# Attention inside a transformer block: scores once in float32 with two heads on the row halves, exponentials transposed by TensorE, values of two heads side by side

## Chip, cores, metric

One core of one Trainium2 chip. The metric is device time in microseconds of one execution, median over runs.

## What is computed

A transformer block with 512 latent and 256 context tokens, width 1024, then a second block (a long convolution and a convolutional feed-forward). The change touches only the attention of the first one, and the retention that is computed beside it. Heads are 64 wide; eight query heads share two key and value heads; retention has eight heads of its own.

```python
def gqa_block(q, k, v):
    qg = q.reshape(B, Q, ATTN_KV_HEADS, GQA_GROUP, HEAD_DIM)
    s = jnp.einsum('bqkgd,btkd->bkgqt', qg, k) * ATTN_SCALE      # HEAD_DIM ** -0.5
    p = jax.nn.softmax(s, axis=-1)
    o = jnp.einsum('bkgqt,btkd->bqkgd', p, v)
...
# retention, per chunk of 128 tokens
inner = jnp.einsum('bhid,bhjd->bhij', qc, kc) * decay_mat
o = jnp.einsum('bhij,bhjd->bhid', inner, vc) + jnp.einsum('bhid,bhde->bhie', qc, state) * q_decay
...
ret = head_group_norm(ret) * silu(g_r)
out = concatenate([att, ret]) @ w_out
```

All is float32. Queries are the 512 latent tokens, keys and values the 768 of context and latent.

## The kernel before

The kernel is written engine by engine, each engine's instructions in an order fixed by hand, with counting semaphores between engines. Features lie on the 128 partitions, tokens along the free dimension. Two heads share one tile `t` (0 to 3): head `h = 2t + e` has the 64 rows `e*64` to `e*64+63`. One of the two (`e = 0`) belongs to the first key head, the other to the second, so `KA` holds both key heads, one on each half of the rows.

Order of the work. The input projection runs 22 units of weights through TensorE (`latent_part`, L638); queries and keys are turned by the rope on VectorE (L2102 to L2111) as their unit comes. Behind it come three things interleaved.

The retention, per pair `t`: `inner(h)` (L842) makes q·k of one head in four products of 128 columns, K = 64 rows, into bank 4 or 5; `ret_decay(h)` on VectorE (L2134) multiplies by the decays into `pr`; `inter(t)` (L855) adds the state's part; `inner_values(t)` (L864) makes the values of head `2t`, then those of `2t+1`, on 64 columns of the array each, into bank 6 or 7. `ret_out` (ScalarE), `gn_variance` (TensorE, L873), `gn_log`, `gn_root`, `gn_gate`, `gn_scale`, `gn_high`, `gn_low` norm, gate and split the result. `query_decay(t)` (VectorE, L2047) prepares `inter`'s operand.

The attention, per head `h`, makes each score twice. `row_max` (L896, L897) makes scores with queries on the partitions, 128 queries by 768 keys, and VectorE takes the largest of each row (`att_max`, L2152). `att_diagonal` and `shift_row` (L907) turn these 512 maxima into a row over all partitions, which `shift_high` and `shift_low` put as a correction into free rows of the query's low part. `scores(h, kt)` (L918, L919) then makes the shifted scores with keys on the partitions, six tiles of 128 keys by 512 queries. ScalarE takes the exponential (`exponent`, L1424) into `PA` or `PB`, and `values` (L931) multiplies by `V`, whose tile has a block of ones beside the 64 value columns, so that the sum of the exponentials comes out on the other half of the partitions. `inverse_sum` (ln and exp on ScalarE) and `att_scale` divide; `att_high` and `att_low` split the result for the output projection.

The products of `row_max` and `scores` are in the float32r type: keys and queries are split into a high part (float32r) and the rest. `Kst` has the high key part on the head's own rows and the low part on the other rows, `K2` the high part and a constant. The splits are made by ScalarE (L1371 to L1388), VectorE (`key_low` L2036, `query_low` L2143 and L2144) and GpSimd (memsets of the free rows). The products of `values`, `inner`, `inter` and `inner_values` are plain float32.

```python
nc.tensor.matmul(PS[:, 4 + kt % 2, :], Kst[:, e, ks], q_high(t, e), start=True, stop=False)
nc.tensor.matmul(PS[:, 4 + kt % 2, :], K2[:, e, ks], q_low(t, e), start=False, stop=True)
...
nc.tensor.matmul(out_bank(h), V[:, kt, h % 2 * HD:h % 2 * HD + P], p_tile(v), start=kt == 0, stop=kt == 5)
```

In the loop over heads TensorE makes `scores` of head h, `values` two tiles behind, and `row_max` of head h+1 between them. VectorE has modulation rows (L2071) in its gaps. The third thing is the output projection with `w_out` (L638 again, eight units), whose first two units start with the slices that are ready; its weights are split by ScalarE (`split_hi`, L621) and VectorE (`split_lo`, L628).

Elsewhere, the filter of the second block has two products on opposite halves of the rows (`filter_tile`, L708 for one tile, L712 for the others), and `key_transposes` (L778) transposes float32 tiles on TensorE.

Of the kernel before, what the change touches and what calls it, by code (L numbers as in the profile page):

```python
# [122 lines left out]
def build(nc, xT, ctxT, cols, mats, w, rope, rdist, crow, mod_x, mod_w, mod_c, posT, fw, fwout, decay, fwd4, inv, out):  # L123
# [3 lines left out]
    with ExitStack() as stack:  # L127
# [45 lines left out]
        Dg = sb("Dg", o_r + 16 * K + LA // P * VW * 4, [P, 4, P])  # L173
# [15 lines left out]
        QS1 = sb("QS1", o_r, [P, 2, 2, L], F32R)  # L189
        R = sb("R", o_r + 8 * K, [P, 2, L])  # L190
        Kst = sb("Kst", o_r + 75 * K, [P, 2, LA], F32R)
        K2 = sb("K2", o_r + 81 * K, [P, 2, LA], F32R)
# [11 lines left out]
        PA = sb("PA", o_r + 38 * K, [P, 6, L])  # L204
        PB = sb("PB", o_t, [P, 6, L])
# [48 lines left out]
        def sem(name):  # L254
# [49 lines left out]
        a_kh, a_kl, a_qh, a_ql = sem("a_kh"), sem("a_kl"), sem("a_qh"), sem("a_ql")  # L304
        a_s, a_mx, a_dg, a_row, a_mh, a_ml = (sem("a_s"), sem("a_mx"), sem("a_dg"), sem("a_row"), sem("a_mh"),
                                              sem("a_ml"))
        a_st, a_exp, a_pv, a_r, a_o, a_h, a_lo = (sem("a_st"), sem("a_exp"), sem("a_pv"), sem("a_r"), sem("a_o"),
                                                  sem("a_h"), sem("a_lo"))
        a_zero = sem("a_zero")
# [137 lines left out]
        def q_high(t, e):  # L447

            return H[:, 0, 2 + e, :] if t % 2 == 0 else QS1[:, 0, e, :]

        def q_low(t, e):

            return H[:, 1, 2 + e, :] if t % 2 == 0 else QS1[:, 1, e, :]

        def p_tile(v):

            return PA[:, v % 12, :] if v % 12 < 6 else PB[:, v % 12 - 6, :]

# [200 lines left out]
        def _(pe):  # L659
# [170 lines left out]
            def inner(h):  # L830

                t, lo = h // 2, h % 2 * HD
                if h == 0:
                    pe.wait_ge(q_done, NROPE - 1)
                elif h == 1:
                    pe.wait_ge(q_done, NROPE)
                else:
                    pe.wait_ge(r_p, h - 1)
                if h % 2 == 0:
                    pe.wait_ge(q_done, rope_count(NQR + t) + 1)  # L840
# [17 lines left out]
            def inner_values(t):  # L858

                for e in range(2):  # L860
                    h = 2 * t + e
                    pe.wait_ge(r_p, h + 1)
                    for c in range(4):
                        mm = nc.tensor.matmul(PS[e * HD:(e + 1) * HD, 6 + t % 2, c * P:(c + 1) * P],  # L864
                                              V[:, c, 3 * HD + h * HD:3 * HD + (h + 1) * HD],
                                              pr[:, h % 2, c * P:(c + 1) * P], start=False, stop=c == 3)
                    mm.then_inc(r_pv, 1)
# [8 lines left out]
            def row_max(h, qt):  # L876

                t, e, u = h // 2, h % 2, 4 * h + qt
                if u == 0:
                    pe.wait_ge(a_kh, 6)  # L880
                if qt == 0:
                    pe.wait_ge(a_zero, h + 1)
                    pe.wait_ge(a_ql, h + 1)
                    pe.wait_ge(a_qh, h + 1)
                if u == 0:
                    pe.wait_ge(a_kl, 2)
                    pe.wait_ge(q_ev, 22)
                elif u == 1:
                    pe.wait_ge(s_st, 8)
                    pe.wait_ge(k_dec, 6)  # L890
                else:
                    pe.wait_ge(a_mx, u - 1)
                qs = slice(qt * P, (qt + 1) * P)
                for a, b, bank in ((0, L, 0), (L, LA, 1)):
                    ps = PS[:, 2 * (qt % 2) + bank, 0:b - a]
                    nc.tensor.matmul(ps, q_high(t, e)[:, qs], Kst[:, e, a:b], start=True, stop=False)  # L896
                    mm = nc.tensor.matmul(ps, q_low(t, e)[:, qs], K2[:, e, a:b], start=False, stop=True)  # L897
                mm.then_inc(a_s, 1)

            def shift_row(h):  # L900

                pe.wait_ge(a_dg, h + 1)
                if h:
                    pe.wait_ge(a_exp, 6 * h - 1)
                else:
                    pe.wait_ge(r_p, 8)
                nc.tensor.matmul(PS[:, 4, :], ones[:, :], Dg[:, :, :].rearrange("p a b -> p (a b)"), start=True,  # L907
                                 stop=True).then_inc(a_row, 1)

            def scores(h, kt):  # L910

                t, e, v = h // 2, h % 2, 6 * h + kt
                if kt == 0:
                    pe.wait_ge(a_ml, h + 1)
                if v >= 2:
                    pe.wait_ge(a_exp, v - 1)
                ks = slice(kt * P, (kt + 1) * P)
                nc.tensor.matmul(PS[:, 4 + kt % 2, :], Kst[:, e, ks], q_high(t, e), start=True, stop=False)  # L918
                nc.tensor.matmul(PS[:, 4 + kt % 2, :], K2[:, e, ks], q_low(t, e), start=False,  # L919
                                 stop=True).then_inc(a_st, 1)  # L920

            def values(h, kt):

                v = 6 * h + kt
                pe.wait_ge(a_exp, v + 1)
                if kt == 0:
                    if h < 2:
                        pe.wait_ge(g_ln, 3 + h)
                    else:
                        pe.wait_ge(a_o, h - 1)  # L930
                nc.tensor.matmul(out_bank(h), V[:, kt, h % 2 * HD:h % 2 * HD + P], p_tile(v), start=kt == 0,  # L931
                                 stop=kt == 5).then_inc(a_pv, 1)

            inner(0)
            inter(0)
            inner(1)
            inner(2)
            inner_values(0)
            inner(3)
            row_max(0, 0)  # L940
            for t in range(1, NPAIR):
                inter(t)
                gn_variance(t - 1)
                if t < 3:
                    inner(2 * t + 2)
                    inner_values(t)
                    inner(2 * t + 3)
                    row_max(0, t)
                else:
                    row_max(0, t)  # L950
                    inner_values(t)
            shift_row(0)
            gn_variance(3)
            row_max(1, 0)
            for h in range(8):
                scores(h, 0)
                scores(h, 1)
                if h < 7:
                    row_max(h + 1, 1)
                for kt in range(2, 6):  # L960
                    values(h, kt - 2)
                    scores(h, kt)
# [1829 lines left out]
```

## Time and profile before

| | |
|---|---|
| device time, three runs | 1436.34 us (1435.34 to 1437.79) |
| span of the profiled execution, first to last instruction | 1433.4 us |
| instructions in it | 16730 |
| TensorE, VectorE, ScalarE, GpSimd busy | 1379.9, 923.8, 536.4, 93.9 us |
| mean granted TensorE clock | 0.989 of full |

The profiled execution's own time is recorded only as its span; the device times of the runs above take in what lies before the first and behind the last instruction. Times in the trace are counted from the start of the span. A product with float32 operands appears as two MATMUL instructions, each with its own weight load (PEld).

### The profile page before, as it was taken

The numbers are of one execution on the slowest core, as the hardware profiler recorded it, in microseconds if no ns is written. First come the engines' busy times: TensorE is split into PE (matmuls) and PEld (weight loads), VectorE is DVE, ScalarE is ACT, GpSimd is POOL, SyncE is SP. The second block draws the span as 40 slices with busy tenths as digits, with TensorE's granted clock in tenths as the row PEclk, the third lists the DMA queues.
The fourth block names the chain that finished last, engine by engine and source line by source line (L and its number), as shares of the span: only waits on it lengthen the run. The fifth ranks groups of instructions, "written<-read, shape, count | busy, mean of one in ns | idle before, by whom it ended". The sixth has DMA issues, their size and how long they took to land.

```text
span 1433.4 us, 16730 instructions
## 1 busy us (share of the span) xinstructions
PE 1379.9 (96%) x6174; PEld 1090.4 (76%) x6174; DVE 923.8 (64%) x1245; ACT 536.4 (37%) x764; POOL 93.9 (7%) x110
## 2 busy tenths in 40 slices
PE   7899999999979999999999999999999999999996
PEld 5688887666748888888887477778887888888885
DVE  6855687785266666655232896999477888785222
ACT  3423353554352232232222654433454333433221
POOL 0002630000300000000110000000110000000010
PEclk9899999999989999999999999999999999999999
DMA  9424330032217666664521021220222322333211
GB/s 383 157 93 153 115 110 23 30 103 89 88 54 247 214 218 214 213 237 172 172 91 63 30 88 65 83 103 30 88 74 82 97 100 88 102 115 105 101 61 59
DMA packets 44801, 168.80 MB, mean 118 GB/s; under 512 B 5547, under 2 KB 6123, under 8 KB 43852
## 3 DMA queue, kind: packets, MB, share of 16 engines
q1 hardware_dynamic: 43340, 165.21, 33.6%
q0 software_dynamic: 1408, 2.89, 0.7%
q8 instruction: 33, 0.54, 0.2%
q14 instruction: 20, 0.16, 0.0%
HBM read 163.09 MB, written 2.10 MB: 115 GB/s over the span
## 4 chain that ended last, share of the span: by engine, by line
PE 84%; DVE 10%; ACT 2%; SPq 2%; issue 1%; DMA 1%; DVEq 0%; ACTq 0%
PE PS L638 68%; PE PS L931 2%; DVE wsp L628 1%; PE PS L1107 1%; DVE tb L1869 1%; DMA wraw<-w_w_in 1%; PE PS L1204 1%; PE PS L1175 1%; PE PS L724 1%; DVE H L1869 1%; PE PS L652 1%; PE PS L896 1%; SPq L516 1%; DVE ca L1869 1%; PE PS L995 1%
## 5 line engine op out<-in xcount | busy, mean ns | idle before, releaser
L638 PE MATMUL PS<-H,wsp 128*128 128x512 f32 x3408 | 786.5, 391 | 12.2 <-DVE wsp L628 8.8
L638 PEld LDWEIGHTS PS<-H,wsp 128*128 128x128 f32 x3408 | 635.9, 188 | 156.5 <-issue 12.0
L628 DVE TENSOR_TENSOR wsp<-wraw,wsp 128x1024 fp32r<-128x1024 f32 (+1 forms) x180 | 233.0, 1295 | 374.8 <-ACT wsp L621 374.1
L621 ACT ACTIVATE wsp<-wraw 128x1024 fp32r<-128x1024 f32 (+1 forms) x180 | 200.5, 1115 | 507.3 <-PE PS L638 494.4
L638 PE MATMUL PS<-hid,wsp 128*128 128x512 f32 x1056 | 240.0, 389 | 0.0
L638 PEld LDWEIGHTS PS<-hid,wsp 128*128 128x128 f32 x1056 | 198.1, 188 | 41.8 <-issue 0.6
L1869 DVE SCALAR_TENSOR_TENSOR cva<-PS,dert,cva 128x441 f32<-128x441 f32 (+2 forms) x176 | 122.2, 695 | 5.5
L2071 DVE CUSTOM_DVE_ANT_0 sink<-mring,crow_t,colt 128x1024 bf16<-128x1024 f32 x56 | 71.7, 1280 | 0.4
L1803 POOL COPY acc<-sqb 128x512 f32<-128x512 f32 x4 | 4.4, 1093 | 867.5 <-ACT sqb L1248 306.9
L1806 POOL TENSOR_TENSOR acc<-acc,sqb 128x512 f32<-128x512 f32 x23 | 40.8, 1773 | 193.7 <-ACT sqb L1781 82.6
L1524 ACT ACTIVATE hid<-hv 128x512 f32 (+1 forms) x22 | 13.9, 632 | 71.3 <-DVE hv L2299 71.3
L2152 DVE TENSOR_REDUCE dert<-PS 128x1 f32<-128x768 f32 x32 | 29.9, 951 | 9.3 <-PE PS L897 9.2
L1760 ACT ACTIVATE sl<-cva,colt 128x512 f32<-128x512 f32 x22 | 15.9, 725 | 50.5 <-DVE cva L1869 50.5
L724 PE MATMUL PS<-sqb,ones 128*128 128x512 f32 (+1 forms) x48 | 26.7, 719 | 7.9 <-ACT sqb L1248 7.9
L1817 POOL DMA_DIRECT2D RS<-RU x44 | 21.8, 502 | 171.9 <-ACT RU L1347 135.5
L1869 DVE SCALAR_TENSOR_TENSOR ca<-cb__148,colt,ca 128x512 f32<-128x512 f32 x40 | 30.0, 749 | 1.2 <-ACT ca L1606 0.5
L638 PEld LDWEIGHTS PS<-Hc,wsp 128*128 128x128 f32 x240 | 30.0, 192 | 0.7
L638 PE MATMUL PS<-Hc,wsp 128*128 128x256 f32 x240 | 30.2, 283 | 0.0
L652 PE MATMUL PS<-H,wsp 128*128 128x512 f32 x96 | 25.7, 429 | 4.1 <-DVE H L1869 4.1
L1869 DVE SCALAR_TENSOR_TENSOR H<-tb,dert,H 128x512 fp32r<-128x512 f32 (+1 forms) x40 | 24.7, 640 | 6.6 <-ACT H L1710 4.1
L1204 PE MATMUL PS<-invt,KS 128*128 128x256 f32 x128 | 28.1, 380 | 0.7 <-DVE KS L2474 0.7
L1248 ACT ACTIVATE sqb<-X 128x512 f32<-128x512 f32 x30 | 18.7, 627 | 26.6 <-DMA X<-xT 9.2
(307 smaller groups left out, 1361.4 us busy)
## 6 DMA issues: line engine op xcount, KB each, us to landing
mring<-mod_c SPq DMA_DIRECT2D x56, 512.0 KB, 4.7
wraw<-w_ffn_in SPq DMA_DIRECT2D x44, 512.0 KB, 3.6
wraw<-w_up SPq DMA_DIRECT2D x44, 512.0 KB, 3.4
wraw<-w_hy_in SPq DMA_DIRECT2D x24, 512.0 KB, 3.4
wraw<-w_w_in SPq DMA_DIRECT2D x22, 512.0 KB, 3.6
wraw<-w_ffn_out SPq DMA_DIRECT2D x16, 704.0 KB, 4.0
wraw<-w_down SPq DMA_DIRECT2D x16, 704.0 KB, 4.1
mfirst<-mod_x SPq DMA_DIRECT2D x12, 512.0 KB, 16.4
```

The lines of the kernel that those rows point to most:

```text
L621: nc.scalar.activation(split_parts(name, i, r)[0], wraw[:, g % RAW, 0:n], ACT.Copy).then_inc(w_hi, 1)
L628: nc.vector.tensor_tensor(part_lo, wraw[:, g % RAW, 0:n], part_hi.bitcast(F32), ALU.subtract).then_inc(w_lo, 1)
L638: mm = nc.tensor.matmul(psum, wsp[:, o % 2, a, wk * P:(wk + 1) * P], h[:, b, kt, :], start=first and kt == kts[0] and (a, b) == (0, 0), st ...
L652: mm = nc.tensor.matmul(psums[u], wsp[:, (o + u) % 2, a, kt * P:(kt + 1) * P], h[:, b, kt, :], start=kt == 0 and (a, b) == (0, 0), stop=kt ...
L724: nc.tensor.matmul(PS[:, bank, 0:n], ones[:, :], sqb[:, q % 2, 0:n], start=kt == 0, stop=kt == KT - 1).then_inc(n_acc, 1)
L931: nc.tensor.matmul(out_bank(h), V[:, kt, h % 2 * HD:h % 2 * HD + P], p_tile(v), start=kt == 0, stop=kt == 5).then_inc(a_pv, 1)
L1204: mm = nc.tensor.matmul(PS[:, inverse_bank(j), par * 256:(par + 1) * 256], spectrum(j // 4, f, a)[:, (j % 4) * P:(j % 4 + 1) * P], invt[:, ...
L1806: PL.tensor_tensor(acc_of(k), acc_of(k), sqb[:, q % 2, 0:n], ALU.add).then_inc(n_acc, 1)
L1817: ins = pool.dma_start(moved_tile(n)[to:to + HALF, :], RU[of:of + HALF, n % 2, 0:L])
L1869: return VE.scalar_tensor_tensor(out=o, in0=a, scalar=s, in1=b, op0=op0, op1=op1)
L2071: VE.tensor_tensor_reduce((sink_w if m - 16 < MOD_W else sink)[:, :], unit, crow_t[:, which, :], 1.0, bias, ALU.mult, ALU.add, to).then_in ...
L2152: VE.tensor_reduce(der("mx", u), PS[:, b:b + 2, :].rearrange("p a b -> p (a b)")[:, 0:LA], mybir.AxisListType.X, ALU.max).then_inc(a_mx, 1)
```

## The change

Scores are made once, with queries on the partitions. There are 16 steps; step `s` is pair `t = s // 4` and one tile of 128 queries, for both heads of the pair. `scores(s)` makes four float32 products of K = 64 rows, alternating between the two halves of the rows, into banks 0 to 3. `att_max` gives the negated maximum, which goes as the bias into the exponential; ScalarE sums the exponentials in the same instruction (`accum_out`). `transposes` turns the 2 x 6 tiles of exponentials by TensorE, four at a time, into bank 4 or 5, from where `evict` copies them to `PT` (ScalarE the first and third four, VectorE the second). `values(s)` multiplies for both heads, alternating between column halves, 12 products of 128 columns. `inverse_row` spreads the reciprocals of the sums over the 64 rows of each head by eight products with the identity; `inverse_copy` and `att_scale` apply them. `inner(t)` and `inner_values(t)` of the retention now take both heads of a pair, alternating as well. The factor 1/8 of the scores is put into the last product of the query's rope. All splits of keys and queries, the shift rows and GpSimd's memsets go. The whole diff of the orders of work is long; its core:

```diff
-            def inner(h):
-                t, lo = h // 2, h % 2 * HD
-                if h == 0:
-                    pe.wait_ge(q_done, NROPE - 1)
-                elif h == 1:
+            def inner(t):
+                if t == 0:
                     pe.wait_ge(q_done, NROPE)
                 else:
-                    pe.wait_ge(r_p, h - 1)
+                    pe.wait_ge(r_p, 2 * t)
                 for c in range(4):
-                    mm = nc.tensor.matmul(PS[:, 4 + h % 2, c * P:(c + 1) * P], KR[lo:lo + HD, t, c * P:(c + 1) * P],
-                                          QR[lo:lo + HD, t, c * P:(c + 1) * P], start=True, stop=True)
+                    for e in range(2):
+                        rows, _ = head_rows(e)
+                        mm = nc.tensor.matmul(PS[:, 4 + e, c * P:(c + 1) * P], KR[rows, t, c * P:(c + 1) * P],
+                                              QR[rows, t, c * P:(c + 1) * P], start=True, stop=True)
                 mm.then_inc(r_s, 1)
...
             def inner_values(t):
-                for e in range(2):
-                    h = 2 * t + e
-                    pe.wait_ge(r_p, h + 1)
-                    for c in range(4):
+                pe.wait_ge(r_p, 2 * t + 2)
+                for c in range(4):
+                    for e in range(2):
...
-            def row_max(h, qt):
...
+            def scores(s):
+                t, qs = step_of(s)
+                if s == 0:
                     pe.wait_ge(q_ev, 22)
                     pe.wait_ge(s_st, 8)
                     pe.wait_ge(k_dec, 6)
                 else:
+                    pe.wait_ge(a_exp, 2 * s)
                 for a, b, bank in ((0, L, 0), (L, LA, 1)):
+                    for e in range(2):
+                        rows, _ = head_rows(e)
+                        mm = nc.tensor.matmul(PS[:, 2 * e + bank, 0:b - a], QA[rows, t, qs], KA[rows, a:b],
+                                              start=True, stop=True)
                 mm.then_inc(a_s, 1)
+            def transposes(s, j):
+                i = 3 * s + j
+                pe.wait_ge(a_exp, 2 * s + (1 if j == 0 else 2))
+                if i < 2:
+                    pe.wait_ge(r_p, 8)
+                elif j == 0:
+                    pe.wait_ge(a_td, s)
                 else:
+                    pe.wait_ge(a_ta, 2 * s + j - 1)
+                for b in range(4):
+                    e, kt = (4 * j + b) // 6, (4 * j + b) % 6
+                    tr = nc.tensor.transpose(PS[:, 4 + i % 2, b * P:(b + 1) * P],
+                                             Pq[:, (2 * s + e) % 4, kt * P:(kt + 1) * P], ident[:, :])
+                tr.then_inc(a_tp, 1)
+            def values(s):
+                t, qs = step_of(s)
+                pe.wait_ge(a_ta, 2 * s + 2)
+                pe.wait_ge(a_td, s + 1)
...
+                for kt in range(6):
+                    for e in range(2):
+                        rows, _ = head_rows(e)
+                        mm = nc.tensor.matmul(PS[rows, 6 + t % 2, qs], V[:, kt, 2 * e * HD:(2 * e + 1) * HD],
+                                              PT[:, s % 2, 6 * e + kt, :], start=kt == 0, stop=kt == 5)
+                mm.then_inc(a_pv, 1)
+            def inverse_row(t):
+                pe.wait_ge(a_rec, t + 1)
...
+                for qt in range(4):
+                    for e in range(2):
+                        rows, _ = head_rows(e)
+                        mm = nc.tensor.matmul(PS[rows, 6 + (t + 1) % 2, qt * P:(qt + 1) * P],
+                                              step_col(2, 4 * t + qt, e).to_broadcast([P, HD]), ident[:, :],
+                                              start=True, stop=True)
+                mm.then_inc(a_row, 1)
...
             inner(0)
+            scores(0)
             inter(0)
             for t in range(1, NPAIR):
+                inner(t)
+                inner_values(t - 1)
                 inter(t)
                 gn_variance(t - 1)
+            inner_values(3)
+            for s in range(NSTEP):
+                if s + 1 < NSTEP:
+                    scores(s + 1)
+                for j in range(3):
+                    transposes(s, j)
+                if s == 0:
+                    gn_variance(3)
+                else:
+                    values(s - 1)
+                    if s % 4 == 0:
+                        inverse_row(s // 4 - 1)
+            values(NSTEP - 1)
+            inverse_row(3)
```

ScalarE and VectorE:

```diff
+            def exponent(s, e):
+                act.wait_ge(a_mx, 2 * s + e + 1)
+                if s >= 2:
+                    act.wait_ge(a_tp, 3 * (s - 2) + 2 + e)
+                SC.activation(Pq[:, (2 * s + e) % 4, :],
+                              PS[:, 2 * e:2 * e + 2, :].rearrange("p a b -> p (a b)")[:, 0:LA], ACT.Exp,
+                              bias=step_col(0, s, e), accum_out=step_col(1, s, e)).then_inc(a_exp, 1)
+            for s in range(NSTEP):                                   # ScalarE
+                evict(s, 0)
+                if s + 1 < NSTEP:
+                    exponent(s + 1, 0)
+                    exponent(s + 1, 1)
+                evict(s, 2)
...
+            def att_max(s, e):
+                dve.wait_ge(a_s, s + 1)
+                VE.tensor_reduce(step_col(0, s, e), PS[:, 2 * e:2 * e + 2, :].rearrange("p a b -> p (a b)")[:, 0:LA],
+                                 mybir.AxisListType.X, ALU.max, negate=True).then_inc(a_mx, 1)
...
             ret_decay(0)
-            query_decay(1)
             ret_decay(1)
-            query_low(0, 0)
+            att_max(0, 0)
+            att_max(0, 1)
             ret_decay(2)
...
+            for s in range(NSTEP):                                   # VectorE
+                if s + 1 < NSTEP:
+                    att_max(s + 1, 0)
+                    att_max(s + 1, 1)
+                evict(s, 1)
...
+                if 1 <= s <= 12:
                     modulation_row(next(mod_next))
```

`query_decay(1)` moves to just behind the last rope product; `split_hi` of w_out's units 0 and 1 to the ends of steps 14 and 15 on ScalarE.

## Rows read from the trace of the kernel before

**Rows 1.** The page, busy time and share of the span of each engine.

```profile
PE 1379.9 (96%) x6174; PEld 1090.4 (76%) x6174; DVE 923.8 (64%) x1245; ACT 536.4 (37%) x764; POOL 93.9 (7%) x110
```

**Rows 2.** Stretches: length, then each engine's busy time, granted clock, DMA.

```profile
227.66:258.25 30.59, 30.33 (x222) 24.87 (x222) 23.33 (x35) 10.58 (x18) 1.04 (x2) 1.00 0.01 2
258.25:349.20 90.95, 89.27 (x317) 54.54 (x316) 67.94 (x94) 49.88 (x84) 2.07 (x4) 1.00 0.23 76
```

**Rows 3.** The chain of waits: start us, us, what.

```profile
236.16 1.78 PE PS L855 x16
...
238.81 1.08 PE PS L842 x8
239.89 1.51 PE PS L864 x16
...
258.51 0.24 PE PS L918
...
260.12 0.86 PE PS L931 x2
...
349.78 10.24 PE PS L638 x45
```

**Rows 4.** Instructions in order of time near 773: start us, us, engine, line.

```profile
772.89 0.59 PE L708 MATMUL PS<-fwo,fz 128*128 128x512 f32 x1
773.41 0.31 PEld L712 LDWEIGHTS PS<-fwo,feat 64*128 64x128 f32 x1 [0.76 <-issue]
773.41 0.82 PE L712 MATMUL PS<-fwo,feat 64*128 64x512 f32 x1
...
773.42 0.81 PE L712 MATMUL PS<-fdif,feat 64*128 64x512 f32 x1
...
774.07 0.59 PE L712 MATMUL PS<-fwo,feat 64*128 64x512 f32 x1
774.07 0.59 PE L712 MATMUL PS<-fdif,feat 64*128 64x512 f32 x1
...
774.59 0.50 PE L638 MATMUL PS<-hid,wsp 128*128 128x512 f32 x1
```

**Rows 5.** Instructions in order of time near 155, TensorE.

```profile
154.68 0.60 PE L778 MATMUL PS<-ident,KR 128*128 128x128 f32 x4
```

**Rows 6.** Groups by line and form, 220 to 352: busy us, mean ns, idle before.

```profile
L2152 DVE TENSOR_REDUCE dert<-PS 128x1 f32<-128x768 f32 x32 | 29.9, 951 | 9.3 <-PE PS L897 9.2
...
L2071 DVE CUSTOM_DVE_ANT_0 sink<-wraw,crow_t,colt 128x1024 bf16<-128x1024 f32 x12 | 15.4, 1279 | 0.2
L1424 ACT ACTIVATE PA<-PS 128x512 f32<-128x512 f32 x24 | 13.9, 598 | 16.2 <-PE PS L919 15.3
...
L2134 DVE TENSOR_TENSOR pr<-PS,Dm 128x512 f32<-128x512 f32 x8 | 5.5, 688 | 4.8 <-PE PS L864 3.1 <-PE PS L842 1.6
...
L1401 ACT ACTIVATE gsq<-PS,colt 128x512 f32<-128x512 f32 x4 | 2.8, 689 | 10.6 <-PE PS L873 10.6
...
L621 ACT ACTIVATE wsp<-wraw 128x1024 fp32r<-128x1024 f32 x2 | 2.1, 1049 | 0.0
...
L2071 DVE DVE_READ_ACCUMULATOR2_ANT dert<- 128x1 f32 x12 | 1.0, 80 | 0.0
```

**Rows 7.** Instructions in order of time, 224 to 230.

```profile
224.42 1.97 PE L759 MATMUL PS<-RU,swap 128*128 128x512 f32 x4
...
227.63 0.95 DVE L2036 TENSOR_TENSOR Kst<-KA,Kst 64x768 fp32r<-64x768 f32 x1
...
227.66 1.16 PE L842 MATMUL PS<-QR,KR 64*128 64x128 f32 x8 [1.26 <-DVE QR L2105]
...
229.94 0.69 DVE L2105 TENSOR_TENSOR QR<-QR,RM 128x512 f32<-128x512 f32 x1
```

**Rows 8.** Stretches as in rows 2, at a long idle stretch of TensorE.

```profile
397.30:401.50 4.20, 0.00 (x0) 0.03 (x1) 2.82 (x5) 2.89 (x4) 0.00 (x0) 1.00 0.00 0
402.40:409.00 6.60, 5.99 (x8) 2.37 (x8) 6.60 (x12) 3.54 (x6) 0.00 (x0) 0.50 0.00 0
```

More of the change, by code:

```diff
@@ L445, in head_rows, with step_of, step_col @@
             return slice(e * HD, (e + 1) * HD), slice((1 - e) * HD, (2 - e) * HD)
[L447 to L457, printed above, removed]
+        NSTEP = 16
+        def step_of(s):
+            return s // 4, slice(s % 4 * P, (s % 4 + 1) * P)
+        def step_col(which, s, e):
+            k = 8 * (s // 4) + 4 * e + s % 4
+            return stat[:, which, k:k + 1]
         def out_bank(t):
@@ L898, in row_max @@
                 mm.then_inc(a_s, 1)
[L900 to L904, printed above, removed]
-                else:
[L906 to L920, printed above, removed]
@@ L952, in _ @@
[L952 to L962, printed above, removed]
-                    if h < 7 and kt < 4:
-                        row_max(h + 1, kt)
-                if h < 7:
-                    shift_row(h + 1)
-                values(h, 4)
-                values(h, 5)
-                if h < 6:
-                    row_max(h + 2, 0)
@@ L1436, in att_high @@
             def att_high(t):
-                act.wait_ge(a_o, 2 * (t + 1))
+                act.wait_ge(a_o, t + 1)
                 SC.activation(H[:, 0, t, :], R[:, t % 2, :], ACT.Copy).then_inc(a_h, 1)
-            query_high(0)
-            for e in range(2):
-                _, other = head_rows(e)
-                SC.activation(K2[other, e, :], KA[other, :], ACT.Identity, scale=0.0,
-                              bias=colt[other, COL["sel"]:COL["sel"] + 1]).then_inc(a_kh, 1)
+            exponent(0, 0)
@@ L1446, in _ @@
+            exponent(0, 1)
             ret_out(0)
@@ L2030, in _ @@
             state_count = [0]
-            def key_low(e):
-                rows, other = head_rows(e)
-                dve.wait_ge(a_kh, e + 1)
-                VE.tensor_tensor(Kst[other, e, :], KA[rows, :], Kst[rows, e, :].bitcast(F32),
-                                 ALU.subtract).then_inc(a_kl, 1)
             def query_decay(t):
@@ L2136, in ret_decay @@
                                  Dm[:, h, :].unsqueeze(1).to_broadcast([P, 4, P]), ALU.mult).then_inc(r_p, 1)
-            def query_low(t, *only):
-                for e in only or range(2):
-                    rows, other = head_rows(e)
-                    dve.wait_ge(a_qh, 2 * t + e + 1)
-                    VE.tensor_copy(q_high(t, e)[other, :], QA[rows, t, :])
-                    VE.tensor_tensor(q_low(t, e)[rows, :], QA[rows, t, :], q_high(t, e)[rows, :].bitcast(F32),
-                                     ALU.subtract).then_inc(a_ql, 1)
```

284 lines of the change are left out of this document (81 added, 203 removed).

## The prediction

> **What bounds the kernel now.** I read the page's busy times first: TensorE is busy for 96% of the span [rows 1], which does not yet say that its work sets the end of this stage. So next the stretches: from the first retention product at 227.66 to the first attention score at 258.25 TensorE is busy 30.33 of 30.59 us, from there to the output projection at 349.20 for 89.27 of 90.95, while VectorE has 67.94, ScalarE 49.88, and the granted clock is 1.00 [rows 2]. Then the chain of waits, which gives a rate for each form. A float32 product comes as two passes: a value product of 512 columns takes 0.86 us (two passes of 0.43), a float32r score product 0.24, the 16 passes of `inter` 1.78, the 8 of one head's `inner` 1.08, the 16 of `inner_values` 1.51 [rows 3]; the shift row and the variance are each one float32 product of 512 columns, 0.86 again. The loop is TensorE's own work: per head 12 score products (2.8 us), 6 value products (5.2), 16 products for the maxima (about 2.7, those of 256 columns at half price) and the row (0.9) make 11.6 us, times 8 is 92 against 91 seen. Hence what matters is the TensorE time of the new loop, and whether another ring becomes longer than it.
>
> **Where the halves stand in the trace.** Two forms decide. For row halves: `filter_tile` (L712) issues two K=64 float32 products on opposite halves of the rows. Their first passes start at 773.41 and 773.42, their second ones both at 774.07 [rows 4]: the two heads together cost what one costs. For column halves: in `inner_values` (L864) the second head follows the first, and 16 passes of 128 columns take 1.51 us where the 16 of L855, on the whole array, take 1.78 [rows 3]: they overlap where the heads meet, though they come one after the other. Alternating, as the change has it, they should overlap throughout. I take full overlap for both. A change of shape costs: L712's first pass is 0.82 us long against 0.59 and its load comes 0.09 after the stream of L708 ends (772.89 + 0.43), so 0.32; back to the full array, from 774.07 + 0.43 to 774.59 plus 0.107 for the first load (128 columns, as long as such a pass), is 0.20 [rows 4]. Into the 128x64 shape I take 0.15 (bounds 0.1 and 0.3).
>
> The Trainium skill (TensorE: Matmul & The Clock Gate, Part 3) says that matmuls start and end strictly in program order. By it the second head's first pass could not start before the first head's second one; the row pair above shows otherwise, so the sum goes by the row, and the rule is a rival below.
>
> **One step of the new loop, on TensorE.** There are 16 steps, each for two heads and 128 queries.
> - Scores: two passes of 512 and two of 256 columns for both heads at once: 2 x 0.427 + 2 x 0.213 = 1.28, with 0.32 to change shape.
> - Twelve transposes. Those of L778 are one pass each, four in 0.60 us with 0.165 of pipeline end, so 0.11 each [rows 5]: 3 x 0.43 = 1.3, with 0.20 to change shape.
> - Values: 12 products, 24 passes of 0.107, two at a time: 1.28, with 0.15.
> - A wait: the third four go to the bank that ScalarE must first clear of the first four. ScalarE's copy is of the length of L1424, 0.60 [rows 6]; with the end of the pipe and a semaphore (0.2) it is done 0.5 to 0.6 after the second four. So 0.55.
>
> Sum 1.60 + 0.20 + 1.3 + 0.55 + 0.15 + 1.28 = 5.1 us.
>
> **The ring beside it.** `scores(s+2)` waits for both exponentials of step s+1, these for the maxima, these for `scores(s+1)`. Counted from the end of the values before: scores done 1.60 + 0.17; the maxima are 0.95 each (L2152), the second ends at 3.65. The exponential of 768 columns is not in the trace: 0.60 for 512 (L1424), 0.22 for 256 more (half of 1.049 - 0.598, L621 with 1024 against L1424), 0.09 for a bias column (L1401 against L1424) make 0.91 [rows 6]. The first starts after ScalarE's copy at 2.95; they follow each other at some 0.8, the pipe's end overlapping, so the second ends at 4.7, and scores could start at 4.75 where values end at 5.1. So 0.35 us of cover. The sum of the exponentials through `accum_out` on ScalarE has no row. Below it is nothing; above it is one more ScalarE instruction of 0.60 each. The nearest kind is VectorE's read of its accumulator, 0.08 (L2071's second row), so I take 0.1 to 0.2 each, which the 0.35 hides. From 0.2 on, every 0.1 adds 0.2 us per step.
>
> VectorE per step: two maxima 1.8, one copy (between 0.60 as ScalarE's L1424 and 0.69 as L2134, both of 512 columns out of PSUM; I take 0.6), a modulation row 1.36, one more 0.69: 4.5 in 5.1, in an order in which the next maximum comes 0.6 later than VectorE is free. ScalarE: 2 x 0.9 + 2 x 0.55 + 0.6 to 1.06 = 4.0. Both lie beside. If VectorE's work grew by more than 0.6, the maximum would be late and the ring with it.
>
> **Loop and its ends.** Step 0 has no values but a variance product: 4.7. Steps 1 to 14: 14 x 5.1 = 71.4. Three inverse rows inside, 16 passes two at a time, 0.86 each: 2.6. Step 15 without scores, the last values and the last inverse row: 0.2 + 0.86 + 0.5 + 0.45 + 0.15 + 1.28 + 1.28 + 0.86 and a change, 5.8. Together 84.5 against 90.95 now. The output projection's first seven slices (42 products at 10.24/45 each, 9.6 us) still cover the last scaling and splitting, about 3 us of four short instructions, and the wait for w_out's third unit comes behind them as before.
>
> **The stage before the loop.** Removed from TensorE: five groups of products for maxima, 5 x 0.7, and the shift row, 1.0. Moved in: `scores(0)`, 1.3. `inner` is now 16 passes with alternating halves; with 128-column passes (0.11 each, L855) the loads may bind: a load of L712 lasts 0.31 beside its twin, where a lone pass waits only 0.11, so loads may share a port [rows 4]. So 1.75 for two heads instead of 2.2 (bounds 0.9 if loads overlap too, and 2.2). `inner_values`: 0.9 plus 0.15 instead of 1.51. Per pair: 1.8 + 1.05 + 1.9 + 0.9 plus changes of shape, about 5.9 instead of 7.2. VectorE's decays (2 x 0.69, L2134) lie under `inter` and the variance product; ScalarE's two exponentials of step 0 run before `ret_out(0)` and end before it is due.
> But the start moves back: `inner(0)` now covers both heads and waits for the last rope product. Without the key split (0.95 at 227.63) that ends 0.95 before 229.94 + 0.69, at 229.7, not 227.66 [rows 7]: 2.0 lost. From there `inner(0)` 1.8, `scores(0)` 1.5, `inter(0)` 1.9, three rounds of 5.9 and `inner_values(3)` 1.2 end at 253.8, so `scores(1)` starts at 254.0, where 258.25 stands now. Gain 4.3, with the 2.0 taken off.
> The key and query splits, memsets, diagonals and shifts leave ScalarE, VectorE and GpSimd; GpSimd's cost nothing, since nothing else waits behind them before the next norm, and the others lay beside TensorE. The scaled last product of the query rope is one instruction as before, at most 0.06 longer, four times, under the projection. No DMA is moved; w_out's first units wait for modulation rows, now one a step up to step 12 and so done near 320, over 10 us before they are needed.
>
> **Sum.** TensorE would start w_out at 254.0 + 84.5 = 338.5, and its first full pass now begins at 349.78 [rows 3]: 11.3 us less. What follows is unchanged. On the profiled span: 1433.4 - 11.3 = 1422.1. That span lies 2.9 below the median 1436.34 of the three runs, so I forecast 1436.3 - 11.3 = 1425.
>
> **The clock.** TensorE would stand idle from 226.4 to 229.7, 3.3 us. In this trace an idle stretch of 4.2 us was followed by 0.50, the lower level of 1.2 GHz, for the whole stretch after [rows 8], while after 1.26 us idle before 227.66 it stayed at 1.00 [rows 2, 7]. 3.3 is between. If the clock falls, half of the 6.6 us that it stayed down there is lost at most: 3.3. I give it 1 in 4; it stays in the forecast's own range, 1420 to 1430.
>
> **Rivals.**
> - The exponentials bound the ring. With 0.5 us for each accumulation a step is 4.6 + 2 x 0.5 = 5.6, 15 x 0.5 = 7.6 more: 1433. Against it is only that the nearest row is short. It would be slower than before above 0.62 each. Chance 0.13, of which 0.08 still ends below 1433.5, 0.02 within 0.2%, 0.03 above.
> - Program order holds between halves. The first long pass of scores then runs alone, 0.43 per step, 6.5 in all: 1431.5. The row pair speaks against it: 0.05. (By that rule of the skill this is what would happen.)
> - The halves do not run side by side in these forms. Scores alone in line cost 1.28 more in each of 16 steps, 20.5: 1445.5; values too: 1466. It decides from 0.7 us lost per step. For it: L842 and L864 show no alternating heads, and the order of issue differs. Against it: rows 3 and 4. Chance 0.10.
> - It does what it says and moves nothing, since something else sets the start of w_out (its weights, VectorE's two splits): 1436. The cover worked out above speaks against it: 0.05.
> - The forecast: 0.67.
>
> Range: the low end is the forecast with loads of `inner` overlapping too (4 x 0.9 = 3.6 less) and a step a tenth shorter; the high end takes in the order rival, most of the exponential rival and no change: 1420 to 1436, with some 0.13 left out. Within 0.2%, 2.9 us, a measurement of this kernel cannot tell from no change. Faster: 0.67 + 0.05 + 0.08 = 0.80; same: 0.05 + 0.02 = 0.07; slower: 0.10 + 0.03 = 0.13.
>
> **What would show it.** Right: L712-like pairs of starts in scores and values, a step of 5.1 us, TensorE waiting some 0.5 us on ScalarE's copy before the third four transposes and nowhere else, `scores(1)` near 254, w_out near 338. Wrong: scores waiting on ScalarE's exponential (accumulation too dear), scores longer than 1.5 or values longer than 1.5 (no overlap), a granted clock of 0.50 behind 229.7, w_out waiting for its weights.

## The result, and the profile after

| | before | changed |
|---|---|---|
| device time, median | 1435.84 us (4 runs) | 1420.72 us (1419.0 to 1421.17, 4 runs) |
| span of the profiled execution | 1433.4 us | 1419.1 us |
| instructions | 16730 | 17635 |

The ratio is 0.9887, 95% interval 0.9875 to 0.9900; the two medians by themselves give 0.9895 and differ by 15.1 us. The forecast was 1425, a ratio of 0.9921 to the 1436.3 it was worked out from, outside that interval. The direction and the loop's mechanism were right; the gain came out a third larger than the 11.3 us forecast, and the time stands at the low edge of the range. The price of `inner` was wrong, as shown below.

The changed kernel's stretches, with the same columns as [rows 2]: TensorE's wait for the last rope product, the time after it at the lower clock, the rest of the stage before the loop, and the loop.

```profile
228.61:231.90 3.29, 0.00 (x0) 0.00 (x0) 3.12 (x6) 0.00 (x0) 0.00 (x0) 0.94 0.00 0
231.98:234.90 2.92, 2.92 (x20) 2.41 (x22) 1.94 (x4) 0.00 (x0) 0.00 (x0) 0.50 0.02 6
234.94:253.70 18.76, 18.76 (x190) 14.75 (x188) 12.14 (x19) 9.21 (x17) 0.00 (x0) 1.00 0.00 1
253.73:336.07 82.34, 76.42 (x763) 55.15 (x763) 61.30 (x88) 53.18 (x108) 0.00 (x0) 1.00 0.29 91
```

The loop is 82.34 us long where [rows 2] have 90.95. The positions cannot be compared directly: in this execution the projection ended 2.2 us later than in that of before, for reasons far ahead of the change. TensorE's first product began at 10.32 instead of 9.44, and the clock was low once more for 3.4 us near 54 us. Counted from the last swap product of the projection (its last pass plus 0.43: 226.2 before, 228.4 after), the loop begins 25.2 us later instead of 32.0, and the loop itself is 8.6 shorter: 15.4 us in all. What comes after w_out's start takes 1084.2 before and 1083.0 after. The marks are good to some 0.4 us: a pass is marked as started while the one before still runs, and by w_out's second pass (349.85 before, 336.34 after) the gain is 15.7.

The chain of waits of the changed kernel, from the rope products to the first step, and one ordinary step. L833 is `inner`, L880 `scores`, L846 `inter`, L856 `inner_values`, L865 the variance, L896 the transposes, L1390 ScalarE's copy, L915 `values`, L929 the inverse row.

```profile
231.98 2.08 PE PS L833 x16
234.06 1.79 PE PS L880 x8
235.85 1.98 PE PS L846 x16
237.83 1.09 PE PS L833 x16
238.92 1.02 PE PS L856 x16
239.94 1.98 PE PS L846 x16
241.93 0.86 PE PS L865 x2
...
283.94 1.49 PE PS L880 x8
285.43 0.60 PE PS L896 x4
286.03 0.02 issue
286.05 0.61 ACT PT L1390
286.66 0.14 issue
286.79 0.63 PE PS L896 x4
287.42 1.46 PE PS L915 x24
288.88 1.49 PE PS L880 x8
```

A step is 288.88 - 283.94 = 4.94 us, 5.1 forecast. `inner` takes 1.09 for two heads, against 1.08 for one in [rows 3]; only the first takes 2.08, at the lower clock. `inner_values` takes 1.02 against 1.51.

Step 0 is the exception: behind it `scores(2)`, at 258.26, follows ScalarE's exponentials in the chain, and step 0 takes 4.53 (4.7 forecast). The last two steps with what follows them take 10.8 (325.25 to 336.07; 10.9 forecast).

The groups that have no row in the trace of before, and the maxima (columns as in [rows 6]):

```profile
L2072 DVE TENSOR_REDUCE stat<-PS 128x1 f32<-128x768 f32 x32 | 29.1, 952 | 17.5 <-PE PS L880 17.5
...
L1380 ACT ACTIVATE Pq<-PS,stat 128x768 f32<-128x768 f32 x32 | 28.4, 899 | 9.5 <-DVE stat L2072 9.5
L896 PE MATMUL PS<-ident,Pq 128*128 128x128 f32 x192 | 27.5, 280 | 5.7 <-ACT PT L1390 5.7
...
L880 PEld LDWEIGHTS PS<-KA,QA 64*128 64x128 f32 x128 | 11.4, 192 | 11.2 <-issue 10.2 <-ACT Pq L1380 1.0
...
L2081 DVE COPY PT<-PS 128x512 f32<-128x512 f32 x16 | 10.9, 680 | 1.5 <-PE PS L896 1.5
...
L1380 ACT ACTIVATION_READ_ACCUMULATOR Pq<-PS,stat 128x1 f32 x32 | 6.6, 205 | 0.0
```

TensorE's idle time in the loop is the wait for ScalarE's copy, 5.7 us in all, some 0.35 in each of 16 steps. The exponential is 0.90 (0.91 estimated), the accumulator costs one more instruction of 0.205 (0.1 to 0.2 taken). The weight loads of `scores` take 0.192 on average: L712's took 0.31 [rows 4], and it was by L712 that I had priced two terms.

### The profile page after: what moved, and what is told of

Its sections match the earlier page's. It is cut to its first block, busy times and chain, and to the rows that moved or that the text cites. A ratio compares the mean times of both kernels' runs of the same rounds, so it can differ in the third digit from the quotient of the medians.

```text
span 1419.1 us, 17635 instructions
## 1 busy us (share of the span) xinstructions
PE 1361.1 (96%) x6606; PEld 1085.9 (77%) x6606; DVE 907.4 (64%) x1227; ACT 531.9 (37%) x778; POOL 89.8 (6%) x102
## 4 chain that ended last, share of the span: by engine, by line
PE 85%; DVE 10%; ACT 3%; issue 2%; DMA 1%; SPq 0%; DVEq 0%; ACTq 0%
PE PS L632 69%; PE PS L880 2%; PE PS L915 2%; DVE wsp L622 1%; PE PS L718 1%; PE PS L896 1%; DVE tb L1808 1%; PE PS L1092 1%; PE PS L1189 1%; PE PS L1160 1%; DMA X<-xT 1%; PE PS L646 1%; DVE H L1808 1%; DVE ca L1808 1%; PE PS L980 1%
## 5 line engine op out<-in xcount | busy, mean ns | idle before, releaser
L632 PE MATMUL PS<-H,wsp 128*128 128x512 f32 x3408 | 787.8, 392 | 12.3 <-DVE wsp L622 8.8
L632 PEld LDWEIGHTS PS<-H,wsp 128*128 128x128 f32 x3408 | 637.0, 188 | 156.6 <-issue 11.1
L632 PE MATMUL PS<-hid,wsp 128*128 128x512 f32 x1056 | 240.0, 389 | 0.0
L632 PEld LDWEIGHTS PS<-hid,wsp 128*128 128x128 f32 x1056 | 198.1, 188 | 41.7 <-issue 0.6
L2072 DVE TENSOR_REDUCE stat<-PS 128x1 f32<-128x768 f32 x32 | 29.1, 952 | 17.5 <-PE PS L880 17.5
L896 PE MATMUL PS<-ident,Pq 128*128 128x128 f32 x192 | 27.5, 280 | 5.7 <-ACT PT L1390 5.7
L1380 ACT ACTIVATE Pq<-PS,stat 128x768 f32<-128x768 f32 x32 | 28.4, 899 | 9.5 <-DVE stat L2072 9.5
L896 PEld LDWEIGHTS PS<-ident,Pq 128*128 128x128 f32 x192 | 20.4, 140 | 14.2 <-issue 14.2
L632 PEld LDWEIGHTS PS<-Hc,wsp 128*128 128x128 f32 x240 | 30.0, 192 | 0.7
L632 PE MATMUL PS<-Hc,wsp 128*128 128x256 f32 x240 | 30.2, 283 | 0.0
```

Of the source, the lines that this page charges most:

```text
L632: mm = nc.tensor.matmul(psum, wsp[:, o % 2, a, wk * P:(wk + 1) * P], h[:, b, kt, :], start=first and kt == kts[0] and (a, b) == (0, 0), st ...
L896: tr = nc.tensor.transpose(PS[:, 4 + i % 2, b * P:(b + 1) * P], Pq[:, (2 * s + e) % 4, kt * P:(kt + 1) * P], ident[:, :])
L1380: SC.activation(Pq[:, (2 * s + e) % 4, :], PS[:, 2 * e:2 * e + 2, :].rearrange("p a b -> p (a b)")[:, 0:LA], ACT.Exp, bias=step_col(0, s, ...
L2072: VE.tensor_reduce(step_col(0, s, e), PS[:, 2 * e:2 * e + 2, :].rearrange("p a b -> p (a b)")[:, 0:LA], mybir.AxisListType.X, ALU.max, neg ...
```

## The experiments

"By stage" below means two durations, read from each profile by the rule used above: from the projection's last swap product to `scores(1)` ("before the loop", 25.2 in the changed kernel), and from there to w_out ("loop", 82.3). Each duration is from one profiled execution. Ratios are to the kernel before, on the same chip.

### Does the overlap hang on the order of issue?

**Scores head by head.** The change's order is undone in one place:

```diff
-                for a, b, bank in ((0, L, 0), (L, LA, 1)):
-                    for e in range(2):
-                        rows, _ = head_rows(e)
+                for e in range(2):
+                    rows, _ = head_rows(e)
+                    for a, b, bank in ((0, L, 0), (L, LA, 1)):
```

> The four score products of a step are issued head by head (head 0: 512 and 256 columns, then head 1) instead of alternating. Alternation theory: the overlap of the row halves hangs on the order of issue; head 1 starts behind head 0's four passes, scores take 1.49 + 1.28 = 2.8 us, a step 6.2 instead of 4.95, the kernel is some 19 us longer (1440). Look-ahead theory: TensorE starts the passes of the other half as soon as they are in its queue, as head 1 of L864 did in the trace of before after five of head 0's eight passes; scores stay within 1.5 to 1.9 us and the time within 0 to 6 us of the changed kernel's 1420.7.

Measured: 1420.05 us, ratio 0.9885 (0.9869 to 0.9902), the changed kernel's. The loop takes 82.4. In TensorE's order of time both heads' first passes are there at once, in one row:

```profile
287.03 0.71 PE L880 MATMUL PS<-KA,QA 64*128 64x512 f32 x2
```

For the scores the order of issue is worth nothing, as the look-ahead theory had it.

**Scores in line.** Head 1 waits for the end of head 0.

```diff
+                    if e == 0:
+                        mm.then_inc(a_half, 1)
+                        pe.wait_ge(a_half, s + 1)
```

> As by head, and head 1 also waits on a semaphore for the end of head 0's last product, so nothing can overlap. Both theories: scores 2 x 1.28 plus the shape change 0.2 plus pipe end and semaphore 0.3, some 3.1 us against 1.49, 16 x 1.6 = 25 us longer, 1446. It prices the overlap of the row halves: if it is well under 25, something else than TensorE sets the step (ScalarE's exponentials end 0.40 before the scores begin, and would then have to be the reason).

Measured: 1449.83, ratio 1.0091 (1.0074 to 1.0108), slower than before. The chain has two pieces where there was one:

```profile
290.96 1.50 PE PS L881 x4
292.46 0.04 issue
292.50 1.55 PE PS L881 x4
```

The loop takes 106.4, 24.1 more. The other 5.0 lie before the loop, where `scores(0)` is in line too and the clock was low for 10.2 us. So the overlap of the row halves, not the order, carries more than the whole gain: without it the change loses.

**Values head by head.** `for e` outside `for kt` in `values`.

> The 12 value products of a step are issued head by head (6 of head 0, then 6 of head 1). Alternation theory: 24 passes of 0.107 in line, 2.57 + 0.15 = 2.7 us against 1.46, a step 6.2, 20 us longer, 1440. Look-ahead theory: head 1 starts after about five of head 0's twelve passes, so (5 + 12) x 0.107 = 1.8 plus 0.15, some 2.0 us against 1.46, 0.5 a step, 8 us longer, 1429.

Measured: 1434.59, ratio 0.9987 (0.9977 to 0.9997), nearly all the gain gone. The chain shows 2.38 us for the 24 passes instead of 1.46:

```profile
290.48 2.38 PE PS L915 x24
```

In equal columns as [rows 2] (TensorE alone), the number of passes under way in the first 0.89 us of them and in 0.41 after:

```profile
290.41:291.30 0.89, 0.89 (x8) 1.00 0.00 0
291.34:291.75 0.41, 0.41 (x10) 1.00 0.00 0
```

Eight passes start in line, one each 0.11. Head 1's first pass (at 291.34, with the longer duration of a first load) starts together with head 0's ninth, when head 0, with 12 passes, has three left to start. From there two start in each 0.11 until head 0 is through, and head 1's last eight are alone again. In L864 of the trace before, of which [rows 3] give only the total of 1.51, head 1 starts with head 0's fifth of eight, again with three left:

```profile
239.82:240.31 0.49, 0.49 (x5) 1.00 0.00 0
240.31:240.69 0.38, 0.38 (x9) 1.00 0.00 0
```

And a head of `scores` has only four passes, so the other starts with its first. One description fits all three: TensorE starts a pass of the other half at most three passes ahead of its turn. Here neither theory's size was right: I expected 5 + 12 slots, it was 8 + 12. For values the alternation is needed and worth 14.2 us of the loop (96.5).

**Retention head by head.** The same in `inner` and `inner_values`.

> Only the retention's products (inner and inner_values) are issued head by head again. My prediction had 1.8 us for an alternating pair of inner because the weight loads were thought to share a port; the trace of after shows 1.09. If the loads of the two row halves run at once only when they alternate, inner goes to 1.09 x 2 = 2.0 and inner_values from 1.02 to 1.5: 4 x 1.4 = 5.7 us longer, 1426. Look-ahead theory: inner loses half of that or less, inner_values 0.4 each: 2 to 4 us longer, 1423 to 1425.

Measured: 1426.69, ratio 0.9924 (0.9907 to 0.9940); before the loop 30.9 instead of 25.2.

```profile
240.12 1.64 PE PS L833 x16
241.76 1.51 PE PS L856 x16
```

1.64 for 1.09 and 1.51 for 1.02: in both, head 1 starts with head 0's fifth of eight passes, three left. Of the 5.7 us, 4 x 1.04 = 4.2 are these. The clock was low for 6.8 us instead of 3.4 in this execution. Values by head above and values between below, whose stage before the loop is the changed kernel's, also had 6.8 us and both took 26.5 there, 1.2 to 1.3 more than 25.2; that accounts for most of the rest.

### What the wait for the rope costs

**Filler.** Three unused products are put into the wait.

```diff
+            pe.wait_ge(q_ev, 22)
+            for x in range(3):
+                nc.tensor.matmul(PS[:, 2, :], ones[:, :], QA[:, 0, :], start=True, stop=True)
             inner(0)
```

> Three float32 products of 512 columns (0.86 each, results never read) are put in front of inner(0), where TensorE waits 3.4 us for the last rope product. Nothing else changes. Clock theory: the half clock that the trace of after shows from 231.5 on comes from that idle stretch; with it filled the granted clock stays 1.00 there, inner(0) takes 1.09 instead of 2.08 and scores(0) 1.49 instead of 1.79, 1.3 us less (1419.4). Rival: the clock falls for another reason or at random; it falls here too, and the time stays at 1420.7.

Measured: 1417.26, ratio 0.9874 (0.9857 to 0.9891). The clock stays up, with TensorE idle for less than 1 us:

```profile
225.50:229.70 4.20, 3.43 (x8) 1.16 (x7) 4.01 (x7) 0.00 (x0) 0.00 (x0) 1.00 0.00 0
229.74:250.00 20.26, 20.26 (x206) 16.02 (x206) 14.13 (x22) 9.16 (x17) 0.00 (x0) 1.00 0.01 2
```

`inner(0)` takes 1.16 and `scores(0)` 1.29 in its chain, 2.45 instead of 3.87; before the loop 23.8, 1.4 less. That is the clock's price. The medians' difference of 3.5 is larger, but the intervals overlap, so it is the 1.4 that I hold to.

**Scores first.** `scores(0)` and `inter(0)` go in front of `inner(0)`.

> scores(0) and inter(0), which need nothing of the last rope product, are issued before inner(0) and fill the idle stretch of 3.4 us. Start theory: 3.4 us of TensorE work move into the gap and the clock stays up; inner(1) then waits about 1.5 us for VectorE's decays, so 3 us less than now (1417.5), scores(1) starts some 3 us earlier after the end of the projection. Rival: the stage before the loop is held by VectorE's order (decays, maxima, query_decay), and under 1 us comes out.

Measured: 1415.34, ratio 0.9865 (0.9845 to 0.9885); before the loop 22.0, 3.2 less, of which 1.4 are the clock's, which stays up here too. The second `inner` now waits for VectorE's decays, 1.3 us:

```profile
228.43 1.98 PE PS L846 x16
230.41 1.12 PE PS L833 x16
231.53 0.02 issue
231.55 1.30 DVE pr L2065 x2
```

### What sets the step

**Values between.** `values(s-1)` goes between the second and third transposes.

```diff
-                for j in range(3):
-                    transposes(s, j)
+                transposes(s, 0)
+                transposes(s, 1)
+                values(s - 1)
+                transposes(s, 2)
```

> values(s-1) is issued between the second and the third four transposes of step s. The wait of 0.54 us for ScalarE's copy is then covered, at the price of one more change of shape, 0.2. Wait theory: a step goes from 4.95 to 4.6, 15 x 0.34 = 5 us less, 1415.6. Ring theory: the exponentials now end 0.40 before the scores start, so the ring of scores, maxima and exponentials is 4.55 us and takes over if anything in it moves later; then a step is 4.6 to 4.8 and 2 to 5 us come out. If the change of shape costs 0.54 or more, nothing does.

Measured: 1418.3, ratio 0.9884 (0.9866 to 0.9901), which by itself shows no gain over the changed kernel. By stage there is one: the loop takes 78.0, 4.3 less. In this execution the clock was low for 6.8 us behind the wait, which made the stage before the loop 1.3 longer, and again for 3.4 us from 345.1 on, behind a wait of 1.8; half of that, 1.7, is an upper bound of what it cost. Together that is up to 3.0 of the 4.3.

```profile
286.16 1.53 PE PS L880 x8
287.69 1.02 PE PS L896 x8
288.71 1.46 PE PS L915 x24
290.18 0.59 PE PS L896 x4
```

A step of 4.60: ScalarE's copy is gone from the chain, and the further change of shape is paid.

**Both.**

> Scores first and values between, together. If the two are independent their gains add: 3 + 5 = 8 us less than the changed kernel, 1412.7. If the ring binds in the loop, the sum is smaller by what the ring keeps: 1414 to 1416.

Measured: 1411.4, ratio 0.9834 (0.9818 to 0.9849), the fastest version here: 24 us under the kernel before, 9 under the changed one by the medians. Before the loop 22.0, loop 78.0: both gains whole, 7.5 us by stage. Scores now follow the last exponential:

```profile
286.01 0.21 ACT L1381 ACTIVATION_READ_ACCUMULATOR Pq<-PS,stat 128x1 f32 x1
286.27 0.30 PEld L880 LDWEIGHTS PS<-KA,QA 64*128 64x128 f32 x4 [0.21 <-ACT Pq L1381]
```

In the changed kernel the same two stand 0.40 apart, and it is the values that scores follow:

```profile
288.20 0.21 ACT L1380 ACTIVATION_READ_ACCUMULATOR Pq<-PS,stat 128x1 f32 x1
...
288.81 0.19 PEld L880 LDWEIGHTS PS<-KA,QA 64*128 64x128 f32 x2 [0.17 <-issue]
```

**More ScalarE, in both kernels.** One copy in front of every exponential from step 1 on.

```diff
+                if s:
+                    own(SC.activation(RS[2][:, 0:256], RS[2][:, 256:512], ACT.Copy))
                 SC.activation(Pq[:, (2 * s + e) % 4, :],
```

> The changed kernel with one more ScalarE copy of 256 columns (some 0.42 us, waited for) in front of every exponential: 0.85 to 0.95 us of ScalarE per step on the ring. Cover theory: 0.40 us of it is hidden, because the exponentials end 0.40 before the scores begin; a step grows by 0.45 to 0.55, 7 to 8 us longer (1428). No-cover theory (ScalarE sets the step already): 13 to 14 us longer (1434).

> The same two copies in the kernel with scores first and values between, whose scores begin 0.05 us after the last exponential. Ring theory: nothing is hidden, a step grows by the whole 0.85 to 0.95, 13 to 14 us more than that kernel's 1411.4 (1425). If TensorE alone set its step of 4.60, as it does in the changed kernel, 0.4 of it would be hidden and it would be 7 longer (1418).

Measured in the changed kernel: 1427.9, ratio 0.9948 (0.9933 to 0.9963), the loop 89.6, 7.3 longer. In the one with both: 1422.96, ratio 0.9913 (0.9898 to 0.9928), the loop 88.7, 10.7 longer. A copy takes 0.41, two in each step. The steps are the same now, 5.50 (284.63 to 290.13) and 5.49 (286.60 to 292.09):

```profile
284.63 1.56 PE PS L880 x8
...
290.13 1.56 PE PS L880 x8
```

```profile
286.60 1.56 PE PS L880 x8
...
292.09 1.56 PE PS L880 x8
```

From 4.94 that is 0.55, from 4.60 it is 0.89. So TensorE set the changed kernel's step with some 0.35 to 0.40 us of cover over the ring of scores, maxima and exponentials, and in the kernel with both no cover is left. Over the loop 13 to 14 were expected in the second and 10.7 came: 15 x 0.89 less 3 x 0.87, the inverse rows inside the loop, which can hide the copies, is 10.7.

### Why the loads were priced too high

**Strided queries.** The queries of a score product are taken four columns apart, which leaves the tokens' results in another order; the kernel leaves out putting them back, so it is good for its time alone.

```diff
-                        mm = nc.tensor.matmul(PS[:, 2 * e + bank, 0:b - a], QA[rows, t, qs], KA[rows, a:b],
+                        mm = nc.tensor.matmul(PS[:, 2 * e + bank, 0:b - a], QA[rows, t, s % 4::4], KA[rows, a:b],
```

> The changed kernel with the queries of a score product taken four columns apart (so the tokens' results stand in another order); the same number of weights is loaded. Stride theory: the 0.31 us of L712's weight loads and its 0.32 us for the change of shape, from which I priced scores and inner, come from its operand being read four columns apart; here the loads of scores go from 0.18 to 0.31 and the first pass begins some 0.1 us later, 0.1 to 0.15 a step, 2 us longer (1422.5). Port theory: loads of two halves share a port whatever the stride; then the loads stay as they are in the changed kernel and so does the time.

Measured: 1422.44, ratio 0.9909 (0.9894 to 0.9924); the loop 84.4, 2.0 more. The loads:

```profile
L880 PEld LDWEIGHTS PS<-KA,QA 64*128 64x128 f32 x128 | 18.8, 312 | 7.7 <-issue 3.2 <-ACT Pq L1380 1.0
```

0.312 against 0.192, L712's figure, and scores of 1.63 instead of 1.49. `filter_tile` reads `feat[half, t:L:4]`. The load's length comes from the stride, not from a port that two halves share: in the changed kernel most loads of `scores` take 0.187 beside their twins, as long as the 0.188 of L632's, which have no twin.

### The retention alone

**The kernel before with `inner` and `inner_values` in pairs,** everything else of the attention as it was.

> The kernel before with one part of the change alone: inner and inner_values of the retention take both heads of a pair, alternating (the order around them as the change has it, the rows of maxima behind inner_values). By the rates seen after, inner 1.09 instead of 2.2 and inner_values 1.02 instead of 1.51, 4 x 1.6 = 6.4 us less, but the start waits for both heads (the two-us later start, and the key split still in front of it) and the clock may fall in that wait: 2 to 4 us of it are given back. So 2 to 4 us less than before (1432 to 1434). If the retention were the greater part of the change's 15 us, it would be 8 or more.

Measured: 1435.23, ratio 0.9995 (0.9986 to 1.0004): nothing. TensorE's order of time:

```profile
232.20 2.08 PE L839 MATMUL PS<-QR,KR 64*128 64x128 f32 x16 [4.29 <-DVE QR L2095]
234.20 3.36 PE L852 MATMUL PS<-QFB,S 128*128 128x128 f32 x16
237.49 1.16 PE L839 MATMUL PS<-QR,KR 64*128 64x128 f32 x16
```

`inner` falls to 1.16 here too. But the wait in front grows from 1.26 [rows 7] to 4.29, 3.0 more, since the pair waits for the last rope product and the key split is still before it. And the clock is low for 6.8 us, the last 4.8 of them behind the wait: the first `inner` takes 2.08 instead of 1.16 and `inter` 3.36 instead of 2.05, 2.2 more. Counted from the projection, the loop begins only 0.3 earlier than in the kernel before. I expected 2 to 4 us to be left. The start and the clock took 5.2 of the 6.4 that I had added up from the rates; where the remaining 0.9 went is not shown.

## Why the prediction came out as it did

- **TensorE sets the loop, before and after.** Right: every piece of an ordinary step of the changed kernel is TensorE's own or the one copy that I had named, and the cover of the ring, 0.35 forecast, is 0.40 in the trace and 0.35 by the two experiments with more ScalarE. Only at step 0 and in the last two steps are ScalarE's exponentials in the chain.
- **The halves overlap, fully where they alternate.** Right, for rows and columns, and it decides the sign: scores in line bring 1449.8. What I had not seen is that scores would overlap in either order.
- **Scores, "with 0.32 to change shape".** Mis-sized. They measure 1.49 with their change of shape, not 1.60. The 0.32 was read from L712, whose loads are slow by their stride. Some 0.11 a step, 1.7 us.
- **`inner`, "the loads may bind", 1.8 us a pair.** This is the step that failed. It is 1.09 at the full clock. I had bounded it from 0.9 to 2.2 and took a value in the upper half, on the ground that a load of L712 lasts 0.31 beside its twin, so that two halves might share a port. The strided experiment shows the 0.31 to be the stride, and the loads do not bind. Four pairs give 2.8 us.
- **Changes of shape between the retention's pieces.** A round is 4.96 (237.83 to 242.79 in the chain), not 5.9: 0.7 of that is `inner`, 0.2 are changes that I added although the pieces of the chain have them in already. Three rounds, 0.7 us.
- **Transposes, the copy's wait, values.** Forecast 0.20 + 1.3 + 0.55 = 2.05 and 1.43; the chain has 2.00 and 1.46.
- **The start.** The pair does begin at the end of the last rope product: 5.2 us after the projection, 5.1 forecast.
- **The clock, "1 in 4".** Too low as a chance. It fell in all eight profiles that have the wait of 3.4 us and in the one with 4.3. Its price, 1.3 to 1.4 us, is less than the bound of 3.3.
- **The two marks of w_out.** The sum sets its 338.5 against 349.78 [rows 3], while its loop of 90.95 us ends at 349.20 [rows 2]. The terms of the sum alone, 4.3 before the loop and 90.95 - 84.5 = 6.4 in it, make 10.7, not 11.3.

Before the loop the gain was 6.8 instead of 4.3: 2.8 for `inner`, 0.7 for the changes of shape, 0.3 in small pieces, less 1.3 for the clock. In the loop it was 8.6 instead of 6.4: 1.7 for the scores and 0.5 in small pieces. That is 4.7 more than the terms had, and 4.1 more than the 11.3 of the forecast. Where the difference went is thus shown by stage. That the forecast came within 4 us is in part luck: the clock and the 0.6 of the marks hid a third of some 6 us that were mis-sized. The low end of the range had been set by just the two things that came, cheaper pairs of `inner` and a shorter step, and the time fell there. None of the rivals came true. Program order did not hold between halves, for rows and for columns.

The Trainium skill (TensorE: Matmul & The Clock Gate, Part 3) has matmuls start strictly in program order. These traces do not agree: with the values head by head, head 1's first value pass at 291.34 starts before three of head 0 that were issued ahead of it. By that rule scores would have taken 0.43 more in each step.

## What to carry to other kernels

Two products on different halves of TensorE's rows or columns cost one, so float32 products, here 0.86 us for 512 columns against 0.24 for float32r [rows 3], can still win if the work comes in such pairs; alternate the halves wherever a half has more than four passes in a row. It is worth adding up where the gain lies. By the rates of the chains, an estimate, scores with maxima and shift rows cost 8 x (2.8 + 2.7 + 0.9) = 51 us before, and scores with transposes 16 x (1.49 + 2.00) = 56 now; values cost 8 x 5.2 = 41 us before, and with the inverse rows 16 x 1.46 + 4 x 0.87 = 27 now. So the values pay for the change, and the scores by themselves are a small loss even with their overlap; no run takes the two apart. When a form is priced from another line of the trace, look at its operand's stride too. And a change that makes two things start together delays the first: fill that wait with work that does not need it, here 3 us for three lines exchanged.

## What the runs showed of the hardware

- TensorE starts a pass of the other half ahead of its turn, by three passes in each case seen (four-pass scores at 287.03, eight-pass retention at 240.31 before, twelve-pass values at 291.34).
- A 64-row weight load of 128 float32 columns takes 0.187 us (median) beside its twin with contiguous columns, and 0.306 with columns four apart.
- ScalarE's accumulation costs a separate instruction of 0.205 us behind each exponential.
- After the same idle stretch of 3.4 us the clock stood at its lower level of 1.2 GHz for 3.4 us in four profiles (the changed kernel, scores by head, strided queries, more ScalarE), 6.8 us in three (values by head, retention by head, values between) and 10.2 us in one (scores in line). Behind w_out's wait of 1.8 us it fell in two profiles of fourteen. The stage before the loop took 25.2 to 25.6 us in the first four and 26.5 in values by head and values between. So one profiled execution of a kernel can differ from another by a us or more in this stage alone, which limits the small comparisons here.
